# Wide up tiles in the first MLP, and the hidden tile's high part written by ScalarE

## The reference

```
def sq_relu_mlp(h, w1, w2):
    return jnp.square(jax.nn.relu(h @ w1)) @ w2

h = modulate(x, sh2, sc2)
x = layer_norm(DEEPNORM_ALPHA * x + g2 * sq_relu_mlp(h, mlp_w1[l], mlp_w2[l]), ln_g[l, 1], ln_b[l, 1])
```

## Time and profile before

| | |
|---|---|
| runs | 1861.44, 1853.84, 1859.19 us; median 1859.19 |
| profiled execution | 1852.43 us, span 1850.6 us |
| PE busy | 1787.8 us (97%), 10814 matmuls |
| PEld busy | 1535.6 us (83%) |
| DVE busy | 1269.0 us (69%) |
| ACT busy | 892.8 us (48%) |
| POOL busy | 1001.9 us (54%) |
| granted TensorE clock, mean | 0.989 of full speed |
| chain that ended last | PE 79%, DVE 12%, DMA 3%, ACT 2%, issue 2%, POOL 1% |

### The profile page before, as it was taken

One profiled execution on the slowest core, in us unless ns is written; L12 is line 12 of the kernel. 1 busy time (PEld: TensorE's weight loads), 2 busy tenths in 40 slices (PEclk: granted clock), 3 DMA queues, 4 the chain that ended last, 5 costly groups with the idle time before them and its releaser, 6 DMA issues.

```text
span 1850.6 us, 30888 instructions
## 1 busy us (share of the span) xinstructions
PE 1787.8 (97%) x10814; PEld 1535.6 (83%) x10814; DVE 1269.0 (69%) x2158; ACT 892.8 (48%) x1507; POOL 1001.9 (54%) x431
## 2 busy tenths in 40 slices
PE   5999899998999999999999999999999999999999
PEld 1847579997978887788868799999999988888887
DVE  6586667878548877433333369988999957777776
ACT  3034654445445554443354546666555555555554
POOL 4033146443775543675438778877776754444443
PEclk7999999999999999999999999999999999999999
DMA  8787247886665554543325455544444455555555
GB/s 322 254 304 252 91 140 243 280 275 220 208 203 182 193 187 160 180 158 110 114 71 172 159 180 182 182 160 161 166 162 151 149 182 193 193 193 193 193 193 169
DMA packets 95322, 346.00 MB, mean 187 GB/s; under 512 B 10544, under 2 KB 12032, under 8 KB 94592
## 3 DMA queue, kind: packets, MB, share of 16 engines
q1 hardware_dynamic: 78048, 283.67, 45.7%
q10 hardware_dynamic: 17184, 61.11, 9.6%
HBM read 343.66 MB, written 1.08 MB: 186 GB/s over the span
## 4 chain that ended last, share of the span: by engine, by line
PE 79%; DVE 12%; DMA 3%; ACT 2%; issue 2%; POOL 1%; DVEq 0%; ACTq 0%; SPq 0%
PE ps L626 29%; PE ps L561 21%; PE ps L573 6%; PE ps L579 3%; PE ps L696 2%; PE ps L782 2%; PE ps L545 2%; PE ps L849 2%; PE ps L796 2%; PE ps L1012 1%; DMA ring<-stream 1%; POOL ring_lo L506 1%; DVE arena L2802 1%; DVE ps L2799 1%; DMA cst<-consts 1%
## 5 line engine op out<-in xcount | busy, mean ns | idle before, releaser
L506 POOL TENSOR_TENSOR ring_lo<-ring,ring_hi 128x1024 fp32r<-128x1024 f32 x371 | 900.1, 2431 | 661.2 <-ACT ring_hi L500 659.7
L500 ACT ACTIVATE ring_hi<-ring 128x1024 fp32r<-128x1024 f32 x502 | 531.8, 1060 | 513.1 <-DMA ring<-stream 510.9
L561 PE MATMUL ps<-h_span,ring_hi 128*128 128x256 f32 x3168 | 416.8, 285 | 0.0
L561 PEld LDWEIGHTS ps<-h_span,ring_hi 128*128 128x128 f32 x3168 | 397.4, 192 | 5.6 <-issue 3.5
L626 PE MATMUL ps<-ring_hi,e_pair 128*128 128x512 f32 x1024 | 253.7, 389 | 0.8 <-DVE e_pair L2830 0.8
L2830 DVE TENSOR_TENSOR e_pair<-arena,e_pair 128x256 fp32r<-128x256 f32 x128 | 174.6, 1364 | 99.0 <-ACT e_pair L1840 98.8
L626 PEld LDWEIGHTS ps<-ring_hi,e_pair 128*128 128x128 f32 x1024 | 192.1, 188 | 41.1 <-issue 1.2
L561 PE MATMUL ps<-h_span,ring_lo 128*128 128x256 f32 x1584 | 222.2, 283 | 0.2 <-POOL ring_lo L506 0.2
L561 PEld LDWEIGHTS ps<-h_span,ring_lo 128*128 128x128 f32 x1584 | 204.3, 192 | 0.4 <-POOL ring_lo L506 0.4
L506 DVE TENSOR_TENSOR ring_lo<-ring,ring_hi 128x1024 fp32r<-128x1024 f32 x141 | 175.6, 1246 | 37.9 <-ACT ring_hi L500 37.7
L626 PE MATMUL ps<-ring_hi,arena_r 128*128 128x512 f32 x672 | 175.5, 394 | 2.2 <-ACT ring_hi L500 2.2
(11 more groups left out here) (301 smaller groups left out, 2268.2 us busy)
## 6 DMA issues: line engine op xcount, KB each, us to landing
ring<-stream SPq DMA_DIRECT2D x540, 512.0 KB, 3.3
arena<-aside_w ACTq DMA_DIRECT2D x49, 512.0 KB, 4.7
late<-aside_w ACTq DMA_DIRECT2D x21, 512.0 KB, 4.4
resid<-aside_w ACTq DMA_DIRECT2D x10, 512.0 KB, 6.3
arena<-scale_w ACTq DMA_DIRECT2D x8, 512.0 KB, 14.9
arena<-ln_rows ACTq DMA_DIRECT2D x8, 512.0 KB, 5.5
arena<-gate_cols ACTq DMA_DIRECT2D x2, 1024.0 KB, 5.3
arena<-decay ACTq DMA_DIRECT2D x1, 1536.0 KB, 6.7
```

Source lines behind the costliest of these rows:

```text
L500: act.activation(ring_hi[:, s, :], ring[:, s, :], ACT.Copy).then_inc(hi_ready, 1)
L506: eng.tensor_tensor(ring_lo[:, s, :], ring[:, s, :], ring_hi[:, s, :], ALU.subtract).then_inc(lo_ready[s], 1)
L561: m = pe.matmul(ps[:, bank, 0:T], w[:, kc * P:(kc + 1) * P], x[:, kc, :], start=begin, stop=w is w_lo and kc == KC - 1)
```

## The change

In mlp0 the up tiles 4 to 31 are made by `h_pair_tile`, as in mlp1; VectorE adds their halves, and ScalarE's and VectorE's lists for mlp0 take mlp1's order, with the aside loads and column sums at the end of a trip. In both MLPs the cast on VectorE goes: ScalarE squares `hid` twice, once into `hid_hi` with rounding and once into `hid2`, and VectorE only subtracts.

```diff
--- before.py
+++ after.py
@@ -1049,10 +1049,7 @@
                 def down_up(j, i=None):
                     wait_hi, wait_lo = hid_waits()
                     rows_unit(u0 + 4 + 2 * j, hid_hi[:, j % 4, :], hid_lo[:, j % 4, :], wait_hi, wait_lo, i, first=j == 0)
-                    if l == 0:
-                        h_tile(u0 + 5 + 2 * j, h_hi_1, 4 + j % 2, i)
-                    else:
-                        h_pair_tile(u0 + 5 + 2 * j, h_parts_1, h_hi_1, 4 + j % 2, i)
+                    h_pair_tile(u0 + 5 + 2 * j, h_parts_1, h_hi_1, 4 + j % 2, i)
 
                 first_tiles(u0, h_hi_1)
                 mark["up", l] = (fills[4].n, fills[5].n)
@@ -1647,6 +1644,12 @@
                 act.wait_ge(hi_ready, SPLIT_NO[u_next + 1])
                 n_norm.add()
 
+            n_relu = Count()
+
+            def squares(j):
+                act.activation(hid_hi[:, j % 4, :], hid[:, j % 4, :], ACT.Square).then_inc(hid_hi_ready, 1)
+                act.activation(hid2[:, j % 4, :], hid[:, j % 4, :], ACT.Square).then_inc(hid_ready, 1)
+
             def mlp(l):
                 u0 = FIRST_UNIT[f"mlp{l}"]
 
@@ -1655,30 +1658,16 @@
                     act.wait_ge(full[b], drains[b].add())
                     act.activation(hid[:, j % 4, :], ps[:, b, 0:T], ACT.Relu).then_inc(emptied[b], 1)
                     act.wait_ge(emptied[b], drains[b].now())
-                    act.activation(hid2[:, j % 4, :], hid[:, j % 4, :], ACT.Square).then_inc(hid_ready, 1)
+                    squares(j)
 
                 unit_hi(act, u0 + 2)
-                if l == 0:
-                    for j in range(31):
-                        hidden(j)
-                        for n in ((3 + j,) if j < 3 else (2 * j, 2 * j + 1)):
-                            unit_hi(act, u0 + n)
-                        if 0 <= j - ASIDE_FROM + 2 < ASIDE_MLP:
-                            aside_load(ASIDE_DONE + j - ASIDE_FROM + 2)
-                    hidden(31)
-                    unit_hi(act, u0 + 62)
-                    unit_hi(act, u0 + 63)
-                    act.wait_ge(aside_done, ASIDE - PAIRED)
-                    norm_rows(1)
-                    return
-                n_relu = Count()
 
                 def summed_hidden(j):
                     b = 4 + j % 2
                     act.wait_ge(emptied[b], drains[b].add())
                     act.activation(hid[:, j % 4, :], hid[:, j % 4, :], ACT.Relu).then_inc(relu_done, 1)
                     act.wait_ge(relu_done, n_relu.add())
-                    act.activation(hid2[:, j % 4, :], hid[:, j % 4, :], ACT.Square).then_inc(hid_ready, 1)
+                    squares(j)
 
                 for j in range(3):
                     hidden(j)
@@ -1686,10 +1675,19 @@
                 hidden(3)
                 unit_hi(act, u0 + 6)
                 unit_hi(act, u0 + 7)
-                for j in range(4, 7):
+                for j in range(4, 31 if l == 0 else 7):
                     unit_hi(act, u0 + 2 * j)
                     unit_hi(act, u0 + 2 * j + 1)
                     summed_hidden(j)
+                    if l == 0 and 0 <= j - ASIDE_FROM + 2 < ASIDE_MLP:
+                        aside_load(ASIDE_DONE + j - ASIDE_FROM + 2)
+                if l == 0:
+                    summed_hidden(31)
+                    unit_hi(act, u0 + 62)
+                    unit_hi(act, u0 + 63)
+                    act.wait_ge(aside_done, ASIDE - PAIRED)
+                    norm_rows(1)
+                    return
                 with rolled(act, 6, [(drains[4], 2), (drains[5], 2), (n_relu, 4)]) as i:
                     for j in range(7, 11):
                         unit_hi(act, u0 + 2 * j, i)
@@ -2398,41 +2396,37 @@
                 for n in range(2, n_tiles):
                     sum_of_halves(dst[:, n, :], 4 + n % 2, first[n % 2] + n // 2)
 
-            def split_hidden(u0):
+            def split_hidden(l):
+
+                u0 = FIRST_UNIT[f"mlp{l}"]
 
                 def up_sum(j, i=None):
                     b = j % 2
-                    sum_of_halves(hid[:, j % 4, :], 4 + b, mark["up", 1][b] + j // 2, i, 2)
+                    sum_of_halves(hid[:, j % 4, :], 4 + b, mark["up", l][b] + j // 2, i, 2)
 
                 def hidden(j):
                     dve.wait_ge(hid_ready, n_hid.add())
-                    dve.tensor_copy(hid_hi[:, j % 4, :], hid2[:, j % 4, :]).then_inc(hid_hi_ready, 1)
-                    dve.wait_ge(hid_hi_ready, n_hid.now())
                     dve.tensor_tensor(hid_lo[:, j % 4, :], hid2[:, j % 4, :], hid_hi[:, j % 4, :],
                                       ALU.subtract).then_inc(hid_lo_ready, 1)
 
                 for j in range(3):
                     unit_lo(dve, u0 + 2 + j)
                     hidden(j)
-                if u0 == FIRST_UNIT["mlp0"]:
-                    for j in range(3, 31):
-                        hidden(j)
-                        unit_lo(dve, u0 + 2 * j)
-                        if 0 <= j - ASIDE_FROM < ASIDE_MLP:
-                            aside_column(ASIDE_DONE + j - ASIDE_FROM)
+                hidden(3)
+                unit_lo(dve, u0 + 6)
+                up_sum(4)
+                for j in range(4, 31 if l == 0 else 7):
+                    unit_lo(dve, u0 + 2 * j)
+                    hidden(j)
+                    up_sum(j + 1)
+                    if l == 0 and 0 <= j - ASIDE_FROM < ASIDE_MLP:
+                        aside_column(ASIDE_DONE + j - ASIDE_FROM)
+                if l == 0:
                     hidden(31)
-                    if 31 - ASIDE_FROM < ASIDE_MLP:
-                        aside_column(ASIDE_DONE + 31 - ASIDE_FROM)
+                    aside_column(ASIDE_DONE + 31 - ASIDE_FROM)
                     unit_lo(dve, u0 + 62)
                     unit_lo(dve, u0 + 63)
                     return
-                hidden(3)
-                unit_lo(dve, u0 + 6)
-                up_sum(4)
-                for j in range(4, 7):
-                    unit_lo(dve, u0 + 2 * j)
-                    hidden(j)
-                    up_sum(j + 1)
                 with rolled(dve, 6, [(n_hid, 4)]) as i:
                     for j in range(7, 11):
                         unit_lo(dve, u0 + 2 * j, i)
@@ -2449,7 +2443,7 @@
             fold(0, 0, SC2, SH2)
             dve.wait_ge(gate_rows_in[0], 16)
             layer_norm(g_rows[0][:, 0, :])
-            split_hidden(FIRST_UNIT["mlp0"])
+            split_hidden(0)
             step(add_bias(1, SH1, 2 * KC, ASIDE - PAIRED))
             settle()
             fold(1, 1, SC1, SH1)
@@ -2500,7 +2494,7 @@
             dve.wait_ge(gate_rows_in[1], 16)
             dve.wait_ge(resid_done, 2)
             layer_norm(g_rows[1][:, 0, :])
-            split_hidden(FIRST_UNIT["mlp1"])
+            split_hidden(1)
             dve.wait_ge(resid_done, 3)
             dve.wait_ge(ln_rows_in[3], 32)
 
```

## The result

The changed kernel takes 1871.7 us (median of 8 runs, 1859.5 to 1877.4) against 1859.0 for the kernel before (8 runs, 1852.9 to 1864.9): ratio 1.0079, interval [1.0058, 1.0100]. It is slower by 0.8%, which lies above the predicted range and on the side of rival B. The profiled execution, 1859.46 us with a span of 1857.6, is the fastest of the eight, so what it shows of the loss is a part; a second trace of the same kernel (the first experiment) is nearer to the median.

The account below looks back on a forecast made before the run. The prediction took TensorE's stream to bound the kernel. Its terms, -3.1 + 0 + 0 + 3.8 + 0.1 = +0.8 us, added to the 1859.2 us median of three runs gave 1860.0 us, range 1852 to 1870.

Parts of the forecast that it names:

- rival B: mlp0's loop: GpSimd's odd-unit rounding holds VectorE's even low parts and TensorE waits; +10.4 to +27 us; chance 0.10.
- Up tiles of mlp0, -3.1: TensorE in mlp0: 28 up tiles with wider matmuls each save 0.11 us, -3.1 us in all.
- The cast's wait passes to the subtraction: VectorE: the subtraction inherits the cast's 1.56 us wait for GpSimd; only the cast's own 0.29 us a tile is won.
- The square and mlp1's loop, 0: ScalarE's second square, 418 ns, stays off TensorE's path in the loops; 0 in mlp1's loop.
- The reduce and the new order in mlp0: mlp0's loop: VectorE gains the reduce, reaching 19.8 us busy of 22, without delaying TensorE; 0 in steady state.
- The price of a collision: mlp0's loop: each low part held by GpSimd makes TensorE wait up to 2.4 us.
- The queues, 0: ScalarE's aside load issues about 1.2 us later, its column sum already done; SP's loads as before; 0.
- The end of mlp0, +3.8: mlp0's last four units: a gap before unit 62's rounding, slow clock and column sum; +3.8 us, between +1.0 and +5.6.
- The end of mlp1, +0.1: mlp1's last four units: VectorE 0.3 shorter, ScalarE 0.4 longer before unit 62's rounding; +0.1 us, between -1.5 and +0.4.
- Rival A: mlp0's end stays near 12.5 us and the loop's gain is kept; -2 to -4 us, about 1856; chance 0.27.
- Rival C: mlp0's loop: transfers set the pace, so the wide tile gains nothing; ends cost 3.9, giving 1863 us; chance 0.08.

Follow-up runs that it names:

- e7: The changed kernel without the 24 aside loads in mlp0, VectorE's column sums kept at full width: 1854.6 us, ratio 0.9988 to the kernel before.
- e8: On top of e5, ScalarE issues each aside load in mlp0 one trip later: 1855.0 us, ratio 0.9983 to the kernel before.
- e1: The changed kernel with mlp0's column sum moved behind the next even unit's low part on VectorE: 1868.4 us, ratio 1.0059 to the kernel before.
- e2_squares: The kernel before with only the second ScalarE square replacing VectorE's cast, in both MLPs: 1853.8 us, ratio 0.9977.
- e0_again: The changed kernel run once more, unedited, for a second trace: 1869.4 us, ratio 1.0070 to the kernel before.
- e10: The changed kernel with only mlp0's aside loads issued one trip later: 1867.2 us, ratio 1.0044 to the kernel before.
- e4: The changed kernel with mlp0's VectorE order subtraction, even unit's low part, sum of halves, column sum: 1868.2 us, ratio 1.0052 to the kernel before.
- e5: On top of e4, both MLP ends round unit 62 before hidden tile 31; mlp0's last column sums come last: 1865.0 us, ratio 1.0043.
- e6_tiny_sums: The changed kernel with mlp0's column sums covering 8 of 1024 elements, aside loads kept: 1860.7 us, ratio 1.0022 to the kernel before.

## Why the prediction was wrong

Point by point, in the order of its steps.

- *Up tiles of mlp0, -3.1*: right. 1.81 + 0.95 a tile; e7 and e8 show the loop at 162.1 where the kernel before had 166.9, 4.8 less, of which 3.1 is the tiles and the rest its two gaps (1.1 idle and 0.27 around each). An estimate from the Trainium skill's N / 2.4 + 2.5 ns (TensorE: Matmul & The Clock Gate, Back-to-back issue gap) would have given 0.6; the trace of after, with 1.81 + 0.95 us a tile, disagrees with it as that of before did.
- *The cast's wait passes to the subtraction*: right. Its median went from 426 to 1666 ns; the forecast was near 1.6 us. e1 adds the column sum, which also has two SBUF inputs and was held for 3.4 us. The traces agree here with the Trainium skill (SBUF — State Buffer, Who interferes with whom): a VectorE instruction with two SBUF inputs contends with GpSimd's reads.
- *The square and mlp1's loop, 0*: right for mlp1's loop, 162.1 in both. For the whole, e2_squares gained some 4 us where 0 was forecast; its profiled trace doesn't show where (loop 167.1), so that cause is open. One thing that its trace does show: without the cast the low part begins 2.60 us after GpSimd's start instead of 2.94, and its shortest spacings, 2.92, hold none.
- *The reduce and the new order in mlp0, "in steady state: 0"*: **this is the step that failed.** It put at nothing what measured 8.5 us of added loop in the profiled execution and 12.4 in e0_again. VectorE's busy share, forecast at 19.8 of 22 us, had room in most windows (17.7 and 18.5 in those above; 21.58 only among the collisions), but what counts is the order: from GpSimd's start to the even unit's low part there are 4.35 us in the trace (2.94 before), and in the trips behind 330 us every odd unit that came sooner than that held a low part, and cost a gap. Rival B said 4.75, counted from the end of the rounding. The prediction had named this as rival B, with its place and its price, and gave it 0.10 because TensorE's own delay was to spread the next units out, and because mlp1 ran without gaps. The first didn't hold: in e0_again six of 24 spacings lie below 4.4 us, and long ones, up to 9.6, stand beside them; and in both traces of this kernel the first held low part in the loop is followed at once by a second (322.94 and 328.32 us in the profile after), though that one cost no further gap. A gap isn't needed for uneven spacings, as e8 has them from 3.21 to 7.67 without one; whether gaps add to them, no run tests. The second left out what mlp0 has and mlp1 has not, the aside loads: with them gone (e7) spacings stay within 5.30 to 5.71 and there is no gap in the loop, as in mlp1.
- *The price of a collision*: from nothing to 2.8 us of TensorE standing, 1.5 on the mean of e0_again's six in the loop, where rival B took 2.4. But a slow clock follows the longest (2.29 and 2.76), and each gap costs 0.27 beside its idle time: divided by the held low parts, the added loop is 12.4 / 6 = 2.1 us in e0_again and 8.5 / 4 = 2.1 in the profile after. TensorE's gaps in mlp0's loop sum to 5.3 and 9.0 us, beyond the 5 that the prediction had named as the sign of B.
- *The queues, 0*: right in the changed kernel (e10 mends nothing), although ScalarE's load did wait for a column sum there once, 5.3 us; in e1, e4 and e5 that wait set the pace. The prediction took the column sum as done by then; that holds only as long as the sum itself isn't held.
- *The end of mlp0, +3.8*: 15.46 - 12.48 = +3.0 in the profiled execution, and +3.1 in e0_again. The size is near, the mechanism is not the forecast one, so that is luck. The forecast had TensorE stand for the rounding of unit 62 behind tile 31. In both traces the large gap (2.09 and 2.18 us) comes earlier and is the lock: TensorE waits for the low part of unit 60, held by GpSimd's of unit 61. The wait for unit 62's rounding is 0.97 us in e0_again and absent in the profiled execution. The slow clock behind the large gap came in the profiled execution alone; in e0_again it stays at 1.00 to the end. The forecast mechanism stands in e7_no_loads, where no low part is held: an end of 16.1 us, near the 16.3 forecast, whose large gap is 2.30 us ahead of the rounded part of unit 62. TensorE's timeline there:

```profile
435.81 1.68 PE L626 MATMUL ps<-ring_hi,arena_r 128*128 128x512 f32 x4 [2.30 <-ACT ring_hi L500]
```

- *The end of mlp1, +0.1*: the gap is 2.18 for 2.17, but the length, said to stay within 0.5 of 15.34, is 13.74 in the profiled execution and 15.82 in e0_again. Behind much the same gap (2.18 and 2.30) the clock stayed at 1.00 in the first and fell to 0.50 for some 3.3 us in the second.
- *Rival A*: mlp0's end didn't stay at 12.5. *Rival C*: refuted by e8's window, 22.00 of 22.00 us busy at 287 GB/s.

In the profiled execution mlp0 is longer by 6.7 us (186.06 against 179.39, from L615 to the idle products) where the prediction had +0.7; in e0_again it is 190.10, +10.7. That is most of the 10.7 to 12.7 between the medians; one trace each can't divide the rest.

## What to carry to other kernels

Where two engines lock each other out, busy shares don't tell whether a list is safe: write down the time from the start of the other engine's instruction to the start of the one that the bound engine needs, and compare it with the shortest spacing of the other engine's starts in the trace, not with the mean. Put that instruction first behind the release of the lock, and work that nobody waits for last; then look whether another engine's in-order list waits for what has been put last, and give that wait a trip of slack. An order copied from a stage that runs well is shown safe only with that stage's transfers.

## What the runs showed of the hardware that was not expected

Not only the subtraction and the low part were held, but the column sum as well, which also has two SBUF inputs: 1.21 us alone, it took up to 3.43 in e1_low_first, and one over 8 elements, 0.15 alone, took 2.17 in e6_tiny_sums. GpSimd is held too: its low part, 2.41 us at the median, took 3.37 in the changed kernel where VectorE's low part had begun 0.11 us before it (394.87 and 394.98), and up to 3.47 beside a column sum recorded 0.02 us later. One line's instructions in the profile after, mlp0 alone:

```profile
L506 POOL TENSOR_TENSOR ring_lo<-ring,ring_hi x30: 2355/2410/3472, 276.8 to 455.8; 128x1024 fp32r<-128x1024 f32 x30
```
